# Attention probabilities transposed by VectorE and a trip through DRAM instead of by TensorE

## The reference

```
s = einsum(q, k) * HD**-0.5 - slope * dist            # dist = q_pos - k_pos
s = where((dist >= 0) & (dist < 128), s, -1e30)
m = max(max(s), sink);  p = exp(s - m)
denom = sum(p) + exp(sink - m)
o = einsum(p / denom, v) * silu(gate)
```

## Time and profile before

| | |
|---|---|
| median of 3 runs | 661.28 us (659.69 to 661.96) |
| the profiled execution | 660.61 us; span from first to last instruction 658.9 us |
| TensorE matmul busy | 653.4 us, 99% |
| VectorE busy | 310.6 us, 47% |
| ScalarE busy | 279.1 us, 42% |
| GpSimd busy | 86.7 us, 13% |
| granted TensorE clock | 1.000 (mean over the span) |

### The profile page before, as it was taken

The page is one execution under the profiler, slowest core; times in us unless marked ns, Lnnn a source line. Parts: engine busy times, 40 slices in busy tenths (PEclk is TensorE's granted clock), DMA queues, the critical chain, the costliest instruction groups (busy, mean ns, idle before and its releaser), DMA issues.

```text
span 658.9 us, 12567 instructions
## 1 busy us (share of the span) xinstructions
PE 653.4 (99%) x4938; PEld 636.6 (97%) x4938; DVE 310.6 (47%) x703; ACT 279.1 (42%) x697; POOL 86.7 (13%) x205
## 2 busy tenths in 40 slices
PE   9999999999999999999999999999999999999998
PEld 8999999999999999999999999999999999999997
DVE  6412453454545768695552587238654761400000
ACT  7573343323234287699555544343533550200000
POOL 0002151424241000000012322232100000000000
DMA  9912304426254402101040201222012532422221
GB/s 335 386 58 97 88 16 171 130 50 155 52 150 112 104 1 65 65 1 64 1 156 12 77 16 68 65 75 65 2 51 78 161 129 78 121 67 66 67 67 34
DMA packets 49206, 58.53 MB, mean 89 GB/s; under 512 B 21016, under 2 KB 42008, under 8 KB 46940
## 3 DMA queue, kind: packets, MB, share of 16 engines
q1 hardware_dynamic: 48716, 57.19, 27.9%
q10 hardware_dynamic: 432, 0.54, 0.2%
HBM read 46.43 MB, written 9.12 MB: 84 GB/s over the span
## 4 chain that ended last, share of the span: by engine, by line
PE 90%; SPq 5%; DMA 4%; issue 1%; DVE 0%; ACT 0%; DVEq 0%
PE proj L496 21%; PE proj L498 20%; PE proj L497 20%; PE branch L498 4%; PE branch L497 4%; PE branch L496 4%; SPq L336 3%; DMA out_s_ret<-s 2%; PE branch L758 2%; PE branch L737 2%; SPq L326 2%; PE branch L692 1%; DMA mixed<-x_first 1%; PE branch L518 1%; PE branch L607 1%; PE branch L642 1%
## 5 line engine op out<-in xcount | busy, mean ns | idle before, releaser
L496 PE MATMUL proj<-big 128*128 128x352 f32 (+1 forms) x912 | 290.0, 318 | 0.0
L498 PE MATMUL proj<-big 128*128 128x352 f32 (+1 forms) x912 | 278.0, 305 | 0.0
L497 PE MATMUL proj<-big 128*128 128x352 f32 (+1 forms) x912 | 277.9, 305 | 0.0
L496 PEld LDWEIGHTS proj<-big 128*128 128x128 f32 x912 | 171.8, 188 | 5.2 <-issue 3.3
L497 PEld LDWEIGHTS proj<-big 128*128 128x128 f32 x912 | 171.9, 188 | 0.2
L498 PEld LDWEIGHTS proj<-big 128*128 128x128 f32 x912 | 171.7, 188 | 0.0
L1292 DVE TENSOR_TENSOR big<-lead,big 128x512 fp32r<-128x512 f32 (+2 forms) x73 | 48.2, 671 | 48.4 <-ACT big L905 48.2
L498 PE MATMUL branch<-m_hi,big 128*128 128x352 f32 x180 | 58.1, 323 | 0.0
L497 PE MATMUL branch<-m_lo,big 128*128 128x352 f32 x180 | 58.0, 322 | 0.0
L496 PE MATMUL branch<-m_hi,big 128*128 128x352 f32 x180 | 57.9, 322 | 0.0
L1796 POOL TENSOR_SCALAR stat<-stat 128x1 f32<-128x1 f32 (+2 forms) x68 | 18.6, 274 | 276.0 <-ACT junk L1074 174.7
(11 more groups left out here) (250 smaller groups left out, 918.9 us busy)
## 6 DMA issues: line engine op xcount, KB each, us to landing
lead<-w_units SPq DMA_DIRECT2D x17, 1024.0 KB, 5.1
xy<-x_T SPq DMA_DIRECT2D x24, 176.0 KB, 2.4
out_y_T<-xy SPq DMA_DIRECT2D x23, 176.0 KB, 1.9
lead<-w_out SPq DMA_DIRECT2D x6, 512.0 KB, 4.0
xy<-w_out SPq DMA_DIRECT2D x6, 512.0 KB, 4.4
mixed<-x_T SPq DMA_DIRECT2D x8, 352.0 KB, 7.9
mixed<-x_prompt SPq DMA_DIRECT2D x5, 512.0 KB, 13.5
s<-state_ret SPq DMA_DIRECT2D x4, 512.0 KB, 4.3
```

Of the source, the lines that this page charges most:

```text
L496: pe.matmul(out, a_lo, b_hi, start=first, stop=False)
L497: pe.matmul(out, a_hi, b_lo, start=False, stop=False)
L498: return pe.matmul(out, a_hi, b_hi, start=False, stop=last)
```

## The change

1. TensorE's `att_turn` goes. VectorE's new `att_turn` transposes `pr` in 32x32 blocks into `pr_blocks`, right after `att_max` of the next tile (slot 6 + 2t).
2. SyncE writes `pr_blocks` to a DRAM buffer `p_way` (four tiles deep), and one step later reads it back in four DMAs into `pr_turned`, 32 partitions each, in pieces of 32 elements (128 bytes), so that each block lands at its transposed place.
3. `att_part`, the product with the masks, goes from VectorE to GpSimd, which reads `pr_turned` in SBUF instead of the bank.
4. `att_values` and `att_mix` come one period later (14 + 2t instead of 12 + 2t).
5. SyncE's stores of the sample keys and values are spread, three to a step, over the steps of the new loop; the weight load of unit 15 (17) and the bias constants of half 1 stand in it at steps 8 and 9.
6. Keys `kT` are kept for one half (with those of the sample tokens apart in `kT_s`), which makes the room for the new tiles. Semaphores of the x loads are shared (`XT_IN`), which makes room for the new ones.

```diff
+            def p_to_way(n8):
+                sp.wait_ge(S_["p_turned"], n8 + 1)
+                sp.dma_start(io["p_way"][n8 % 4], pr_blocks[:]).then_inc(S_["p_out"], 16)
+
+            def p_from_way(n8):
+                sp.wait_ge(S_["p_out"], 16 * (n8 + 1))
+                if n8 >= 2:
+                    sp.wait_ge(S_["pT_set"], n8 - 1)
+                way = io["p_way"][n8 % 4].rearrange("(r a) (g c b) -> c a g r b", r=4, g=2, c=4)
+                for c in range(4):
+                    sp.dma_start(pr_turned[32 * c:32 * c + 32, n8 % 2, :].rearrange("a (g r b) -> a g r b", g=2, r=4),
+                                 way[c]).then_inc(S_[f"p_placed{n8 % 2}"], 16)
...
             for half in range(2):
                 if half:
-                    sp.wait_ge(S_["biased"], 8)
-                    sp.dma_start(cc[:, C_BIAS:N_CC], io["c_att"][:, N_CC:N_CC + 4 * P]).then_inc(S_["cc_in"], 16)
...
-                    for b in range(DB):
+                for j in range(3, NT + 4):
+                    if j < NT + 3:
+                        p_to_way(8 * half + j - 3)
+                    if j > 3:
+                        p_from_way(8 * half + j - 4)
+                    for i in range(3 * (j - 3), min(3 * (j - 2), 2 * DB)):
+                        b, n9 = i // 2, 9 * half + NT
                         rows = slice(b * DS, (b + 1) * DS)
...
+                    if j == NT:
+                        load_w(15 + 2 * half)
+                    if j == NT + 1 and half == 0:
+                        sp.wait_ge(S_["biased"], 8)
+                        sp.dma_start(cc[:, C_BIAS:N_CC], io["c_att"][:, N_CC:N_CC + 4 * P]).then_inc(S_["cc_in"], 16)
...
-            def att_turn(half, t):
-                n8 = 8 * half + t
-                pe.wait_ge(S_["pr_set"], n8 + 1)
-                if n8 > 0:
-                    pe.wait_ge(S_["pT_set"], n8)
-                for g in range(2):
-                    mm = pe.transpose(bb[2][:, g * P:(g + 1) * P], pr[:, n8 % 2, g, 0:P], ident[:])
-                mm.then_inc(S_["pT_done"], 1)
...
                 act.wait_ge(S_["kT_done"], n9 + 1)
-                act.activation(kT[:, half, chunk_cols(t)], bb[0][:, 0:n], ACT.Copy).then_inc(S_["kT_set"], 1)
+                if half and t == 0:
+                    act.wait_ge(S_["sc_done"], NT)
+                out = kT[:, chunk_cols(t)] if t < NT else kT_s[:, half, :]
+                act.activation(out, bb[0][:, 0:n], ACT.Copy).then_inc(S_["kT_set"], 1)
...
-            def att_part(half, t):
+            def att_turn(half, t):
                 n8 = 8 * half + t
...
+                dve.wait_ge(S_["pr_set"], n8 + 1)
+                if n8 > 0:
+                    dve.wait_ge(S_["p_out"], 16 * n8)
+                dve.transpose(out=pr_blocks[:], in_=pr[:, n8 % 2, :, 0:P]).then_inc(S_["p_turned"], 1)
...
+            def att_part(half, t):
+                n8 = 8 * half + t
+                pool.wait_ge(S_[f"p_placed{n8 % 2}"], 64 * (n8 // 2 + 1))
...
+                if n8 >= 2:
+                    pool.wait_ge(S_["av_done"], n8 - 1)
+                k0 = 1 if t == 0 else 0
+                shape = (P, 2 - k0, 2, P)
+                pool.tensor_tensor(pT[:, n8 % 2, 2 * P * k0:].rearrange("p (k g i) -> p k g i", k=2 - k0, g=2),
+                                  pr_turned[:, n8 % 2, :].rearrange("p (g i) -> p g i", g=2).unsqueeze(1).to_broadcast(shape),
+                                  pmask[:, k0:, :].unsqueeze(2).to_broadcast(shape), ALU.mult).then_inc(
+                                      S_["pT_set"], 1)
...
             for half in range(2):
                 for j in range(NT + 1):
+                    if half == 1 and j < 4:
+                        att_part(0, j + 4)
                     n, n9 = tile_rows(j), 9 * half + j
                     pool.wait_ge(S_["k_ss"], 2 * n9 + 1)
...
                     if j < NT:
                         sink_column(half, j)
+                    if j >= 5:
+                        att_part(half, j - 5)
+            for t in range(4, NT):
+                att_part(1, t)
```

More of the change, by code:

```diff
@@ L70, in done @@
     return sum(UNITS[u][0] not in TOKEN_MAJOR or j < NT for u, j in GROUPS[:g + 1])
+XT_IN = (("xt_in0", 16), ("xt_in1", 16), ("xt_in2", 16), ("x_in0", 32), ("x_in1", 32), ("x_in2", 32), ("x_in3", 32),
+         ("x_in12", 32), ("x_in4", 32))
 X0_IN = ("x_in0", "x_in1", "x_in2", "x_in3", "x_in12")
@@ L220, in layer @@
             sb("mixed_c", [P, 3 * H, TOK], scope=r)
-            kT = sb("kT", [P, 2, TOK], scope=r)
+            kT = sb("kT", [P, SEQ], scope=r)
+            kT_s = sb("kT_s", [P, 2, NS], scope=r)
             v_c = sb("v_c", [P, 2, NT + 1, DH], scope=r)
@@ L228, in layer @@
             biased_row = sb("biased_row", [P, 4 * P], scope=r)
+            pr_blocks = sb("pr_blocks", [P, 2 * P], scope=r)
+            pr_turned = sb("pr_turned", [P, 2, 2 * P], scope=r)
             pT = sb("pT", [P, 2, 4 * P], scope=r)
@@ L420, in _ @@
                         continue
-                    for b in range(DB):
-                        rows = slice(b * DS, (b + 1) * DS)
-                        store(io["s_k"][b, WINDOW - DS:WINDOW, half], kn[rows, n9 % 2, :], "stored_kv")
-                        store(io["s_v"][b, WINDOW - DS:WINDOW, half], v_c[rows, half, t, :], "stored_kv")
-                load_w(15 + 2 * half)
+                for j in range(3, NT + 4):
[5 more added lines that the diff above has]
+                        b, n9 = i // 2, 9 * half + NT
+                        rows = slice(b * DS, (b + 1) * DS)
+                        if i % 2:
+                            store(io["s_v"][b, WINDOW - DS:WINDOW, half], v_c[rows, half, NT, :], "stored_kv")
+                        else:
+                            store(io["s_k"][b, WINDOW - DS:WINDOW, half], kn[rows, n9 % 2, :], "stored_kv")
+                    if j == NT:
[3 more added lines that the diff above has]
+                        sp.dma_start(cc[:, C_BIAS:N_CC], io["c_att"][:, N_CC:N_CC + 4 * P]).then_inc(S_["cc_in"], 16)
             sp.wait_ge(S_["w_hi_set"], PIECES * NU)
@@ L777, in samp_scores @@
                         q = qT[:, (9 * half + NT) % 2, NS * b:NS * b + NS]
-                        mm = pe.matmul(bb[4][32 * c:32 * c + 32, P:P + NS], q, kT[:, half, SEQ:TOK], start=False,
+                        mm = pe.matmul(bb[4][32 * c:32 * c + 32, P:P + NS], q, kT_s[:, half, :], start=False,
                                        stop=(e == 1), skip_group_check=True)
@@ L806, in att_side @@
                     att_q(9 * half + (s - 3) // 2)
-                if s % 2 == 0 and 0 <= (s - 12) // 2 < NT:
-                    att_values(half, (s - 12) // 2)
+                if s % 2 == 0 and 0 <= (s - 14) // 2 < NT:
+                    att_values(half, (s - 14) // 2)
                 if s % 2 == 0 and 0 <= (s - 4) // 2 < NT:
                     att_scores(half, (s - 4) // 2)
-                if s % 2 == 0 and 0 <= (s - 8) // 2 < NT:
-                    att_turn(half, (s - 8) // 2)
                 if s == 21:
@@ L1667, in att_side @@
                     att_probs(half, (s - 6) // 2)
-                if s % 2 == 0 and 0 <= (s - 12) // 2 < NT:
-                    att_mix(half, (s - 12) // 2)
+                if s % 2 == 0 and 0 <= (s - 14) // 2 < NT:
+                    att_mix(half, (s - 14) // 2)
                 if s % 2 == 0 and 0 <= (s - 4) // 2 < NT:
                     att_max(half, (s - 4) // 2)
-                if s % 2 == 0 and 0 <= (s - 8) // 2 < NT:
-                    att_part(half, (s - 8) // 2)
+                if s % 2 == 0 and 0 <= (s - 6) // 2 < NT:
+                    att_turn(half, (s - 6) // 2)
                 if s == 17:
```

32 lines of the change are left out of this document (12 added, 20 removed).

## The result

| | before | after |
|---|---|---|
| median (4 runs each) | 660.88 us (659.69 to 661.96) | 666.81 us (666.40 to 668.60) |
| the profiled execution | 660.61 us | 666.74 us |
| its span | 658.9 us | 664.9 us |
| granted TensorE clock | 1.000 | 0.997 |

The ratio is 1.010 (95% interval 1.0084 to 1.0116). I forecast 660.2 us and a range of 657.0 to 665.5: the time lies outside it, on the slow side.

What follows compares the result with a forecast made beforehand. TensorE, busy 653.4 of 658.9 us, was taken as the bound. Transposes removed, -3.5, plus key waits, +2.4, gave -1.1 us: 659.5 for the profiled execution, 660.2 for the median, range 657.0 to 665.5 us.

Steps and rivals of the forecast that it cites:

- the place and the mechanism: Unit 14's key transposes: key roots stand behind mask products waiting for reads, so TensorE waits 0.7, 1.3 and 0.4 us.
- Rival 1: Key transposes of unit 14: no wait at all, all 3.5 us kept, 657.8 us; chance 0.28.
- rival 2: SyncE's 128-byte reads from DRAM are dear to issue or land, giving 670 or 668 us; chance 0.17.
- Rival 3: VectorE's queue: waiting for the write's landing makes VectorE fall behind, about +3 us, 663.5 us; chance 0.08.
- what is saved: TensorE loses 32 probability transposes, 16 pairs at 0.22 us each: 3.5 us less.
- the prices of the parts: Off TensorE: reads issue in 0.61 and land in 2.0 us, mask product 1.2 us, 256-column VectorE transpose 0.43 us.
- Values in time: TensorE's value products: tightest at tile 2 of half 0 with slack 1.0 us, so 0 us wait, bounds 0 to 1.
- SyncE just keeps up: SyncE's issuing in the attention loop: a step of 4.0 us against a period of 4 to 5 us.
- keys ready 413.1 ... waits 0.4: Third key transpose of unit 14: keys ready at 413.1, TensorE comes at 412.7, so it waits 0.4 us.
- The clock needs no term: TensorE's granted clock: 1.0 over the span before the change, so no time was added for it.
- The range: Whole kernel, 8 in 10: 657.0 to 665.5 us; key waits up to 6.5 us with reads landing in 4.4 us.
- Half 1: Units 16 and 17: no key roots behind mask products; ScalarE loses about 0.5 us, hidden from TensorE, so 0.

Runs made afterwards that it cites:

- the small stores first: Kernel after, with SyncE's 16 small stores of each half ahead of its loop instead of three per step: 664.14 us, ratio 1.0050.
- the late load alone: Kernel after, with only unit 15's weight load moved behind the reads of tile 7 and its splits to later slots: 664.47 us, ratio 1.0063.
- the third root first: Kernel after, with only tile 6's mask product in unit 14 moved behind the key root of its step on GpSimd: 662.42 us, ratio 1.0025.
- the two orders mended: Kernel after, with unit 14's key roots ahead of the mask products on GpSimd and small stores ahead of SyncE's loop: 657.63 us, ratio 0.9962.

## Why the prediction was wrong, step by step

**Right: the place and the mechanism.** The waits are at unit 14's key transposes, and the cause is the mask products ahead of the key roots on GpSimd; undoing only that order gives back 6.5 us. Rival 1 (no wait) and rival 2 (dear reads) fall. Rival 3's mechanism, VectorE held up by the landing of a write, is there with 4.3 us in three waits, but it is one link in the same chain and comes to TensorE through the same key norms.

**Right: what is saved.** 3.5 us forecast for the pairs of transposes; put back as idle ones they cost 3.66 us of device time, 2.65 of them inside the span. In the trace, TensorE is 1.5 us ahead of the kernel before when unit 14 begins (396.0 against 397.5), and from its last key transpose (439.1 against 431.7) to the end it gains a further 1.3 us.

**Right: the prices of the parts.** Lines 355 and 1857 (issue ns or duration; then time to landing):

```profile
L355 SPq DMA_DIRECT2D pr_turned<-p_way x64: 557/613/1667, 380.5 to 490.0; - x64
...
DMA to landing us min/median/max: 2.0/2.2/5.0
```

```profile
L1857 POOL TENSOR_TENSOR pT<-pr_turned,st_tails x16: 739/1283/1532, 384.9 to 492.1; 128x512 f32<-128x512 f32 x14, 128x256 f32<-128x256 f32 x2
```

Issue 0.61 and landing 2.2, forecast 0.61 and 2.0 from the earlier trace rows; product 1.28, forecast 1.2 from two small shapes; block transpose 0.435 us, forecast 0.43. The reads from DRAM are hardly dearer than the SBUF rows by which I priced them, which settles rival 2. The Trainium skill (DMA: Bandwidth & Descriptors, why small descriptors are slow) says that transfers between SBUF and SBUF are spared the penalty of small pieces; for these 32 KB reads from DRAM in 128-byte pieces no more than 0.2 us of it shows in the landing (2.2 us, against 2.0 in the earlier trace rows, medians).

**Nearly right: "Values in time".** The term was 0, with bounds of 0 to 1 us. The two weight loads above waited 0.6 us together for mask products of half 0. The 0.4 us at a value product in half 1, which the profile gives to its own issue, ended at 466.68, and GpSimd ended that tile's mask product just before, at 466.6, so it too was most likely a wait for the product:

```profile
465.30 1.28 POOL L1857 TENSOR_TENSOR pT<-pr_turned,st_tails 128x512 f32<-128x512 f32 x1 [0.79 <-DMA pr_turned<-p_way]
```

**Failed: "SyncE just keeps up".** I set a step of 4.0 us of issuing against a period of 4 to 5 and called it even. It counted every issue at its median. The timeline has four reads in 3.59 us instead of 2.6, a first store behind them of 0.50 instead of 0.30, and at tile 5 SyncE is 1.2 us behind (turned 397.5, written 398.68); with VectorE's stall before (1.28 us, a write of 3.5) the load left 2.4 us later than I had it. The keys for the first transpose were ready at 405.7 where I had 403.5 (its terms add up to 403.35); TensorE came for them at 403.7 where I had 402.8. With the stores out of the way the waits are 0.68 and 1.46, against 0.7 and 1.3 forecast. In the kernel after they are 2.11 and 2.04. Why the write of tile 4 took 3.5 us rather than 1.7 stays open.

**Failed, and the largest: "keys ready 413.1 ... waits 0.4".** The third term followed the keys to the key transpose and stopped there. In the kernel before, VectorE's timeline has, behind the third key norm,

```profile
410.92 0.35 DVE L1546 SCALAR_TENSOR_TENSOR kn<-proj,stat,gain 128x128 f32<-128x128 f32 x1 [1.11 <-POOL stat L1797]
411.18 0.68 DVE L1292 TENSOR_TENSOR big<-lead,big 128x512 fp32r<-128x512 f32 x1
...
412.43 0.30 DVE L1654 TENSOR_SCALAR kcT<-kcT,stat 128x160 f32<-128x160 f32 x1
```

and TensorE transposed that `kcT` 0.4 us after its end:

```profile
413.13 0.27 PE L784 MATMUL branch<-ident,kcT 128*128 128x128 f32 x1
```

The slack of the third key norm was thus 0.4 us, by way of the sample probabilities, and not the 2.1 us from its end to its own transpose at 413.35. I had asked what waits for the norm, not what stands behind it in VectorE's queue. To that comes the price of L1666 itself, 0.78 us where it was 0.30 (its other execution took 0.304): it ran while GpSimd made the mask product of tile 7 (416.52 to 418.03). The wait at this place, forecast as 0.4 us, was 2.3 us in the kernel after and 5.4 us when it stood alone, and moving that one product gave back 4.4 us.

**Failed: "The clock needs no term".** This was read from a kernel without pauses and carried to one that I had just given 2.4 us of them. The clock cost 1.5 us here. It fell in this stretch in the profiles of seven kernels, whose longest wait there was 2.2 to 5.4 us (the kernel after and six of the experiments), and stayed at 1.00 in the four whose longest was at most 1.3 us. It is no fixed price. All four executions of the kernel after show the fall in their mean clock (0.995 to 0.997), but with the small stores first it shows in six of nine executions (medians 664.4 us with it, 662.8 without), with the late load alone in one of four, and with the third root first in three of seven, where it cost nothing.

**The range.** Its upper end for the key waits was reads that land in 4.4 us, 6.5 us in all. The waits were indeed 6.4, but that is luck: only the reads of tile 5, issued beside the weight load, landed in 4.3 us; those of tiles 4 and 6 took 2.1 and 2.5 (medians of four), and other causes made their waits. The clock put 1.5 on top. That case gives -3.5 + 6.4 + 1.5 = +4.4, 665.7 on the median of before, just above my end of 665.5. The 1.1 us from there to the 666.8 measured are of the size of the scatter at L569 (0.9).

**Half 1** came out as forecast: from 424 us on TensorE's only wait is the one of 0.4 us.

## What to carry to other kernels

When an instruction that waits for a DMA is put into an engine's program, list everything behind it on that engine, then everything behind *those* on the next engine, and take the least slack of the whole list; here it was 0.4 us, two engines away. The DMA-issuing engine here, whose step at median prices equalled the period, was late, so give such a step some slack. A pause put into TensorE can cost its length plus the clock that goes with it: put a term for it into the upper end of the range. Before giving a change up, look at the order alone: with the two orders mended the same change was 2.5 us faster than the kernel before instead of 6 us slower.

## What the runs showed of the hardware

- A write of 128 KB that lands in 1.7 us alone took 5.3 us beside a load of 1 MB, whether the load stood ahead of it on the same queue (5.24) or was issued 0.46 us earlier on another engine's queue (5.3). A second queue gave a small transfer no way past a large one.
- Pauses of TensorE can be dearer than their length. After waits of 2.1, 2.0 and 2.3 us within 15 us the granted clock was 0.50 for about 3.4 us, which cost 1.5 us. In some executions of other kernels with a wait of 2.2 us or more in their profile the mean clock stayed at 0.999 or 1.000. Why it fell behind the first wait of 2.3 us in the kernel with the third root first, and not behind the first of 2.1 us in the kernel after, isn't settled.
- Now and then one DMA issue in a group of four reads took 1.35 us (at most 1.67) in place of 0.61, and the first small store behind such a group 0.50 in place of 0.30. No run here says why.
- GpSimd's product with two SBUF inputs (1.28 us) slowed VectorE's instructions beside it: a scaling took 0.78 instead of 0.30, and a merge of `pr` (L1616, 0.43 by its median) 0.92 us while the mask product of tile 3 ran. The Trainium skill (SBUF — State Buffer, on the port pair shared by the two engines) says that one instruction holds the pair and the other is blocked; the trace agrees in that both VectorE instructions ended only after the GpSimd product beside them (418.12 against 418.03, and 400.64 against 400.36), though less behind it than a whole one of them takes alone (0.30 and 0.43).
